# A two-block model on one core: gather waves, a gated convolution and softmax choice, before and after a reordering of the gather phase

## The reference

```python
def ada_params(cond, w, b):                       # 48 + 48 columns of w @ silu(cond)
    return jnp.split(jax.nn.silu(cond) @ w + b, 6, axis=-1)

def conformer_conv(h, ...):
    a = h @ w_pw1 + b_pw1
    a = a[..., :d] * jax.nn.sigmoid(a[..., d:])
    a = depthwise_conv_31_taps(a) + b_dw
    a = jax.nn.silu(layer_norm(a, g_ln, b_ln))
    return a @ w_pw2 + b_pw2

def peer_ffn(h, w_query, sub_keys, u_tab, v_tab):  # per token, 8 heads
    q = h @ w_query                                # two halves per head
    s_top, i_top = lax.top_k(q . sub_keys, 16)     # of 128 keys, both halves
    best, pos = lax.top_k(s_top[0] + s_top[1], 16) # of 256 pairs
    expert = i_top[0] * 128 + i_top[1] at pos;  gate = softmax(best)
    act = gelu(u_tab[expert] . h)
    return sum(gate * act * v_tab[expert])         # 16 experts a head
```

## Time and profile before

| | us |
|---|---|
| three runs, median | 3035.68 |
| three runs, lowest to highest | 3028.53 to 3036.81 |
| the profiled execution, its own time | 3033.09 |
| its span, first to last instruction | 3031.3 |
| PE, DVE, ACT, POOL busy | 2421.9, 1897.2, 1402.2, 641.6 |
| moved by DMA | 855.92 MB |

### The profile page before, as it was taken

One profiled execution on the slowest core, in us unless ns is written; L12 is line 12 of the kernel. 1 busy time (PEld: TensorE's weight loads), 2 busy tenths in 40 slices (PEclk: granted clock), 3 DMA queues, 4 the chain that ended last, 5 costly groups with the idle time before them and its releaser, 6 DMA issues. The chain is left out here.

```text
span 3031.3 us, 42342 instructions
## 1 busy us (share of the span) xinstructions
PE 2421.9 (80%) x14174; PEld 1576.2 (52%) x14174; DVE 1897.2 (63%) x4413; ACT 1402.2 (46%) x3482; POOL 641.6 (21%) x600
## 2 busy tenths in 40 slices
PE   7989765655777766767855555899999999998998
PEld 3534632311444422534511110699858989985798
DVE  1866357576664666676577776566746666675565
ACT  3245243333664435654444443445635454464544
POOL 0400143443223434233344444000000000000000
PEclk9989887866878877988977677799999999999999
DMA  9940899999978999888999999555425555552454
GB/s 313 375 153 1 293 418 419 418 420 420 352 273 330 400 419 419 329 316 310 398 420 420 421 420 421 213 184 177 157 70 174 186 159 185 184 163 80 148 184 151
DMA packets 159313, 855.92 MB, mean 282 GB/s; under 512 B 17713, under 2 KB 17841, under 8 KB 92721
## 3 DMA queue, kind: packets, MB, share of 16 engines
q0 software_dynamic: 85392, 579.38, 47.6%
q1 hardware_dynamic: 72000, 261.73, 25.6%
q10 hardware_dynamic: 1760, 12.75, 1.2%
HBM read 852.73 MB, written 1.05 MB: 282 GB/s over the span
## 5 line engine op out<-in xcount | busy, mean ns | idle before, releaser
L1831 PE MATMUL ps<-arena 128*32 128x512 f32 x1232 | 390.9, 776 | 321.8 <-ACT arena L1185 311.2
L2229 DVE TENSOR_TENSOR w_lo<-weights,w_hi 128x512 fp32r<-128x512 f32 x528 | 364.3, 691 | 280.8 <-ACT w_hi L979 278.8
L979 ACT ACTIVATE w_hi<-weights 128x512 fp32r<-128x512 f32 x528 | 333.0, 632 | 375.3 <-PE ps L1785 278.8
L899 POOL DMA_INDIRECT arena<-experts,arena x308 | 347.9, 1129 | 723.3 <-PE ps L1831 519.9
L2477 DVE SCALAR_TENSOR_TENSOR arena<-arena 128x1024 f32<-128x1024 f32 x308 | 370.9, 1225 | 201.1 <-DMA arena<-experts,arena 198.7
L1831 PE MATMUL ps<-held,arena 128*32 128x512 f32 x816 | 265.5, 779 | 201.4 <-ACT arena L1185 192.2
L1783 PE MATMUL ps<-a_hi,w_hi 128*128 128x256 f32 x1408 | 399.8, 284 | 5.8 <-DVEq L2248 2.7
L1785 PE MATMUL ps<-a_hi,w_lo 128*128 128x256 f32 x1408 | 398.9, 283 | 0.0
L1784 PE MATMUL ps<-a_lo,w_hi 128*128 128x256 f32 x1408 | 398.9, 283 | 0.0
L1177 ACT ACTIVATE arena<-arena 128x1 f32<-128x1 f32 x512 | 101.7, 199 | 627.9 <-DVE arena L2477 368.7
L1831 PEld LDWEIGHTS ps<-arena 128*32 128x32 f32 x1232 | 51.3, 121 | 537.2 <-ACT arena L1185 505.5
(11 more groups left out here) (275 smaller groups left out, 3927.3 us busy)
## 6 DMA issues: line engine op xcount, KB each, us to landing
weights<-stream SPq DMA_DIRECT2D x497, 512.0 KB, 3.9
arena<-mod_rows_in POOLq DMA_DIRECT2D x64, 512.0 KB, 9.7
mod_rows<-mod_rows_in POOLq DMA_DIRECT2D x16, 512.0 KB, 13.8
arena<-experts,arena POOLq DMA_INDIRECT x308, 17.5
held<-experts,arena POOLq DMA_INDIRECT x204, 17.5
arena<-gain_rows ACTq DMA_DIRECT2D x1, 3072.0 KB, 11.9
arena<-rpb_windows ACTq DMA_DIRECT2D x4, 512.0 KB, 15.6
arena<-keys_in ACTq DMA_DIRECT2D x2, 1024.0 KB, 9.6
```

Source lines behind the costliest of these rows:

```text
L899: pool.indirect_dma_start(out=pair_of(k), out_offset=None, in_=experts[k // PICKS], in_offset=bass.IndirectOffsetOnAxis(ap=expert[:, at:at ...
L979: act.activation(w_hi[:, o % 2, part], weights[:, t.unit, part], ACT.Copy).then_inc(hi_ready, 1)
L1831: ins = pe.matmul(ps[first:first + WAVE, v % 2, :], diag[:, k % DIAGS, :], v_of(k, HALF * half, HALF * (half + 1)), start=(k % WAVE_PICKS ...
L2229: dve.tensor_tensor(w_lo[:, o % 2, part], weights[:, t.unit, part], w_hi[:, o % 2, part].bitcast(F32), ALU.subtract) \
```

## The change

- Rows: all 80 rows of the ada weights are taken during attention (`MOD_ROWS`), and the two late slots go.
- Pick: the gate is put into the mask once a group (`gated`, 128x512, on DVE in `settle`), so ACT has two instructions a pick instead of three. PE takes two picks at a time, at odd beats.
- Choice: `choose` stands in three pieces, two beats apart; its pairs of 128x256 instructions become single ones of 128x512.
- Gate of the convolution: the sigmoid is `0.5*tanh(x/2)+0.5`, one ACTIVATE and a scaling.
- Norms: the late norms are one multiplication of DVE over all chunks, and ACT puts in gain and shift in one instruction. `fold` has two instructions instead of eight, `spread` one. ACT evicts `pw2` instead of DVE.
- Convolution blocks: 160 and 96 columns go in (128 and 128 before), 128 and 128 come out (96 and 160 before), at beats 162 and 258. Five chunks are on PE and three on DVE, three instructions a beat instead of eight. `pw1` is every two beats instead of every three.

```diff
-ROW_RING, EARLY_ROWS, LATE_ROWS = 7, 66, 14
+ROW_RING, MOD_ROWS = 7, 80
-GLU_COLS = [slice(0, 128), slice(128, 256)]
-OUT_COLS = [slice(0, 96), slice(96, 256)]
+GLU_COLS = [slice(0, 160), slice(160, 256)]
+OUT_COLS = [slice(0, 128), slice(128, 256)]
-PW1_ORDER = [4, 0, 1, 5, 2, 3, 6, 7]
-TAPPED = [4, 5, 6, 7]
-DIRECT = [(0, 1), (2, 3)]
+PW1_ORDER = [3, 0, 1, 2, 4, 5, 6, 7]
+TAPPED = [3, 4, 5, 6, 7]
+DIRECT = [(0, 1, 2)]
+DIRECT_PART = 1
+CONV_BEATS = (162, 258)
+GLU_STEP = 2
...
 # scalar engine, pick(k)
-                    act.wait_ge(gelu_done, k + 1)
-                    act.activation(act_w[:, one], act_out[:, one], ACT.Copy, scale=gate[:, one]).then_inc(weighed, 1)
-                    act.wait_ge(weighed, k + 1)
                     if k >= DIAGS:
                         act.wait_ge(v_used, k - DIAGS + 1)
-                    act.activation(diag[:, k % DIAGS, :], const("token"), ACT.Copy, scale=act_w[:, one]) \
+                    act.wait_ge(gelu_done, k + 1)
+                    act.activation(diag[:, k % DIAGS, :], gated_token(k), ACT.Copy, scale=act_out[:, one]) \
...
 # scalar engine, pw1(b, c)
-                    act.activation(sig[:, n % 2, :], bank(pr)[:, P:2 * P], ACT.Sigmoid,
-                                   bias=col("b_pw1", 8 + c)).then_inc(sig_ready, 1)
+                    act.activation(t, bank(pr)[:, width(cols_of):2 * width(cols_of)], ACT.Tanh, scale=0.5,
+                                   bias=half_bias[:, c:c + 1]).then_inc(glu_tanh, 1)
+                    act.wait_ge(glu_tanh, n + 1)
+                    act.activation(t, t, ACT.Copy, scale=0.5, bias=0.5).then_inc(sig_ready, 1)
...
 # tensor engine, at odd beats
+                def pick_pair(k):
...
+                    for one in (k, k + 1):
+                        pe.wait_ge(diag_ready, one + 1)
+                        pe.wait_ge(pair_landed[one % PAIR_RING], landed(one))
+                    for one in (k, k + 1):
+                        for half in range(2):
+                            first = WAVE * (2 * (one % 2) + half)
+                            ins = pe.matmul(ps[first:first + WAVE, v % 2, :], diag[:, one % DIAGS, :],
+                                            v_of(one, HALF * half, HALF * (half + 1)), start=(k % WAVE_PICKS == 0),
+                                            stop=(k % WAVE_PICKS == WAVE_PICKS - 2), skip_group_check=True)
+                        ins.then_inc(v_used, 1)
...
 # vector engine, attn()
-                row_dots(46, 66)
+                row_dots(46, 74)
                 dve.wait_ge(table_loaded, 16)
                 head_apply(2)
+                row_dots(74, MOD_ROWS)
...
 # vector engine, settle(c)
-                    dve.tensor_tensor(part, part, R["inv"].to_broadcast([P, TOPK]), ALU.mult).then_inc(gate_set, 1)
+                    dve.scalar_tensor_tensor(out=gated[:, c % 2], in0=part.unsqueeze(2).to_broadcast([P, TOPK, WAVE]),
+                                             scalar=R["inv"], in1=const("token").unsqueeze(1).to_broadcast([P, TOPK, WAVE]),
+                                             op0=ALU.mult, op1=ALU.mult).then_inc(gate_set, 1)
```

More of the change, by code:

```diff
@@ L210, in gather_order @@
             put("scores", c, pe=-1, act=-1)
-            put("choose", c, dve=c - 1)
+            for part in range(3):
+                put("choose", c, part, dve=c - 1)
             if c == 0:
@@ L222, in gather_order @@
         put("query", 0, 1, m, pe=20 + 4 * m, act=21 + 4 * m)
[L223 to L231, removed]
-        for i, c in enumerate(PW1_ORDER):
[L233 to L238, removed]
+    put("late_mods", 0, dve=22)
@@ L248, in gather_order @@
-        put("var_root", b, act=last + 5)
-        put("spread", b, dve=last + 6, act=last + 7)
+            put("tap_out", b, c, act=first_tap + parts * (n + 1) + 1)
+        for n, group in enumerate(DIRECT):
+            first = glu + GLU_STEP * max(PW1_ORDER.index(c) for c in group) + 3 + n * DIRECT_BEATS
+            for i, part in enumerate(range(0, TAPS, DIRECT_PART)):
+                put("direct", b, n, part, dve=first + i)
+        last = max(first + i, first_tap + parts * len(TAPPED) + 1)
@@ L250, in gather_order @@
+        put("mean", b, pe=last, dve=last + 1)
+        put("var", b, act=last + 2, pe=last + 2)
+        put("var_root", b, act=last + 3)
+        put("spread", b, dve=last + 4, act=last + 5)
         for m in range(KC):
[L251 to L254, removed]
+            put("pw2", b, m, pe=last + 6 + m, act=last + 7 + m, dve=last + 8 + m)
@@ L260, in gather_order @@
         beat = TOPK * (c - 1)
-        late = 3 if c == GROUPS + WAVE_GROUPS * 3 else 0
+        late = LATE_GROUPS.get(c, 0)
         put("scores", c, pe=beat - 6 + late, act=beat - 4 + late)
-        put("choose", c, dve=beat + 1)
-        put("exps", c, act=beat + 6)
+        for part in range(3):
+            put("choose", c, part, dve=beat + 1 + max(late - 4, 0) + 2 * part)
+        put("exps", c, act=beat + 6 + max(late - 4, 0))
     for v in range(ALL_WAVES):
@@ L664, in bass_two_blocks @@
         row_landed = [sem(f"row_landed{r}") for r in range(ROW_RING)]
-        late_landed = [sem(f"late_landed{r}") for r in range(2)]
         row_dot = sem("row_dot")
@@ L902, in gather @@
                         .then_inc(pair_landed[k % PAIR_RING], 16)
-                    for what, *which in ORDER["pool"].get(k, ()):
-                        steps[what](*which)
             for name, k in phases:
@@ L1232, in conv_squares @@
                 def conv_squares(b):
-                    for v in range(WAVES // 2):
-                        wait_taken(act, pl["fold", WAVES // 2 * b + v])
+                    for v in range(GLU_COLS[b].start // WAVE, GLU_COLS[b].stop // WAVE):
+                        wait_taken(act, pl["fold", v])
                     square_block(f"conv{b}")
@@ L2541, in direct @@
                     chunks, out_cols = DIRECT[n], OUT_COLS[b]
-                    for j in range(part, min(TAPS, part + TAP_PART)):
+                    for j in range(part, min(TAPS, part + DIRECT_PART)):
                         for c in chunks:
```

205 lines of the change are left out of this document (112 added, 93 removed).

## The result

| | before | after |
|---|---|---|
| runs, median | 3034.43 us (4 runs, 3028.53 to 3036.81) | 2916.37 us (4 runs, 2913.66 to 2921.97) |
| ratio to before | | 0.9616, 95% interval 0.9595 to 0.9638 |
| span of the profiled execution | 3031.3 us | 2912.3 us |

A forecast was written before the change was run, and what follows sets the result against it. DMA at 418 to 421 GB/s bounds most of the gather, with two dips losing 117.2 us. 3033.1 - 17.5 (rows) - 91 (dips) - 0.7 (last fold) = 2923.9, 2926 us by median; own range 2908 to 2946, 8 in 10: 2900 to 2962.

The forecast's parts named there:

- Step 1: 14 ada rows leave the gather phase, where DMA is the bound: 17.5 us less transfer, at its full price.
- Step 2: The 14 rows' dots go into two DVE gaps in attention: cost 0, up to 17.5 us if that cover failed.
- Step 3: In the convolution blocks DVE's 4.06 us a pick falls to 2.7 to 2.9; short only by some 8 us.
- rival C: Tanh needs its own table, so table loads stay and only the DVE part is won: 2957, at worst 2980; chance 0.04.
- Step 4: Gate's table loads go and all 80.1 us of DVE's sigmoid wait; PE late by 8 and 2 us in the blocks.
- Step 5: Norm and `pw2` chain, 44 us of DVE's waiting a block: some 8 us a block left, bounds 0 and 25.
- Step 6: Pairs of picks on PE: the even slot waits up to 2.50 us more, hidden where DMA bounds; no gain counted.
- Step 7: Fold, choice and mask get shorter but are off the path; only the last fold counts, 0.7 us less.
- A: DMA bounds throughout and the queue hides all that is left, so all 117 us are won: 2901 us; chance 0.17.
- B: Half the dips' loss stays, 60 us instead of 26; waits move to PE's chunk and the norms: 2960; chance 0.20.
- D: The rows in attention aren't hidden: +17.5 us eats what taking them out of the gather gives, 2944; chance 0.05.
- E: Slower: the gather's ring of ten slots runs dry everywhere, 0.3 us a pick over 400 picks: 3046; chance 0.04.

## Why the prediction was right, and where its steps were not

- Step 1 (rows out of the gather, -17.5): right, 17 to 20 measured by putting them back.
- Step 2 (rows in attention, 0): right in the cost; 0.6 us late at both gaps, nothing left at the first gather. The gaps of 9.54 and 7.21 us are now filled down to 2.43 and 0. That the first gap is late by about the 0.5 forecast is chance: the dots ended 2.43 us ahead of ACT, and ACT itself was late.
- Step 3 (DVE is short of time in the blocks; by rival C half of the loss is its part): failed as a cause on its own. The 4.06 us a pick stand for a beat with eight taps, but by the counts of the earlier trace rows (120 + 120 instructions, eight a beat) there are only 30 such beats, 15 a block. Together they are 30 x (4.06 - 2.50) = 47 us too long at most, in pieces that the queue can take up, and the run with the old places shows 7 to 9 us in the new surroundings.
- Step 4 (80 us of sigmoid wait gone, PE left with 8 + 2): half right. The wait came 14 times and not 16. The loads went (30, not the 32 of the sum) and none came for the tanh (rival C is out), but 34.7 of 80.1 us of waiting stayed, and by itself the tanh brought 25 us in before and at most some 5 to 7 in after. I had read the releaser (ACT 1250) as the cause. With the single picks at 1.05 us a pick, which the pairs halve, there was as much to win at PE: in the kernel before the pairs alone take as much off this wait as the tanh alone.
- Step 5 (chain, 8 us a block left): too high, by how much isn't known. In the two windows together 14.3 us of transfer are idle for all reasons, where steps 4 and 5 left 10 + 16 = 26, and the runs don't say how the 14.3 split. The steps made shorter were worth 12 us. But the wait at the `pw2` part did not get shorter by going to ACT (18.7 to 17.9).
- Step 6 (pairs: the even slot later, hidden, no gain): the cost was right, 417 GB/s in the long stretch even with eight slots. The gain was overlooked: 33 us in before, 21 in after. Step 4 had the duration right as one of two cases (1.05 for a pair) but priced it only as something that might go wrong later.
- Step 7 was too small for any run to show.

The signs went the same way. The rates of the blocks, the attention, ACT's table loads and the long stretches came as foretold. Three did not: the gate's product waits 34.7/16 = 2.2 us on average where at most 1 was to be seen, the last dot is 120.7 us earlier and not 105 to 115, and the hundredth dot 24.7 (644.4 against 669.1 us) and not some 17, though the 97th is 18.0 earlier.

So the sum came out within 10 us because 117.2 us, what the dips could give at most, came from the windows of before, and because I took nearly all of it as won, which it was. That part was sound. That the causes inside were misjudged and the sum still held is luck: a gain put at nothing (the pairs) stood in for one priced too high (DVE's load, and the whole of the sigmoid's wait). The 10 us that are off are the idle transfer, 14.3 in place of 26, less the 1.7 us given back behind the gather. Of the rivals, A (2901) has none left, so the truth lies midway between it and the forecast, nearer than its 0.17 said. B (coupling stays, 60 us left, 2960) comes near to the kernel before with tanh and pairs alone, which has 70 left. C is out by the tanh without a load, D by the attention timeline, E by the long stretches, at 416 to 418 GB/s.

## What to carry to other kernels

Where a queue has dips, take the most that can be won from the rate in windows, and trust that more than the list of waits: the wait that is longest on one engine names the engine that came last, not the one that made it late. Here the longest wait named ACT, and pairing the matmuls of PE took as much off it as removing ACT's table loads. When several engines pass each item on in order, a part's worth depends on what else is there (25 us for the tanh in one kernel, some 5 to 7 in the other, if anything), so try each part both ways, alone on the old kernel and taken out of the new one. Where matmuls fill only two of the four column groups of 32, it is worth trying to issue them for two items at a time: here the second item was free or nearly so.

## What the runs showed of the hardware

- Column groups side by side: two groups, 4 matmuls of 512 columns, 1.03 to 1.05 us; four groups, 8 matmuls, 1.04 us. A single record reads a little longer (838 against 772 ns), the sum over all picks much shorter (389.5 against 670.2 us with single picks in the changed kernel).
- With the pairs PE was less busy and had a lower granted clock, and no cost of it is to be seen: in 1475 to 1790 us PE is busy for 131 of 315 us at 0.57 (1.2 GHz, the lower level, would be 0.50), with single picks for 197 at 0.69; DMA moves 417 and 421 GB/s, and 420 in two other kernels with pairs at 0.57. The busy time alone doesn't say the clock: the kernel before has 190 us at 0.75 there.
- Tanh ran between gelus without a table load. ACT's timeline in the first block of after (1186 the gelu, 1266 the tanh), where neither the tanh nor the next gelu has a load ahead of it:

```profile
838.49 0.19 ACT L1186 ACTIVATE arena<-arena 128x1 f32<-128x1 f32 x1
838.76 0.32 ACT L1192 ACTIVATE arena<-gated,arena 128x32 f32<-128x32 f32 x1
838.99 0.38 ACT L1266 ACTIVATE arena<-ps,small 128x160 f32<-128x160 f32 x1
839.40 0.34 ACT L1269 ACTIVATE arena<-arena 128x160 f32<-128x160 f32 x1
...
841.27 0.19 ACT L1186 ACTIVATE arena<-arena 128x1 f32<-128x1 f32 x1
```

  The Trainium skill (ScalarE: Activation LUTs, "Table sets: the hidden batching unit") lists tanh with the exp and sigmoid sets, and the row of the gelu set doesn't name it. The trace adds what that row leaves out: one loaded set served both.
- The weight tiles wait beside the gather: PE's wait for the stream grows from 0.4 us in before to 9.2 with single picks in the changed kernel and 25.3 in after. Why was not tried.
